# Transposes between the products of the phase that reads them, and attention output scaled by heads on VectorE alone

## The reference, cut to what matters

```
h = rmsnorm(x) * (1 + scale1) + shift1
q_r, k_r, v_r, g_r, q_d, k_d, v_d, gate_r, gate_d = split(h @ w_in)      # gates: sigmoid
branch_r = (silu(g_r) * group_norm(retention(q_r, k_r, v_r))) @ w_ret_out
o_d      = rmsnorm_per_head(diff_attention(q_d, k_d, v_d))               # 8 heads of 128
branch_d = o_d @ w_diff_out
x  = x + gate1 * ((gate_r * branch_r + gate_d * branch_d) @ w_o)
h2 = rmsnorm(x) * (1 + scale2) + shift2
x  = x + gate2 * ((silu(h2 @ w_ffn_gate) * (h2 @ w_ffn_up)) @ w_ffn_down)
y  = rmsnorm(x)
```

## Time and profile before

| | us |
|---|---|
| median of 3 runs | 1375.28 |
| the profiled execution's own time | 1375.61 |
| its span (first to last instruction) | 1373.9 |
| TensorE matmul busy | 1307.0 (95%) |
| VectorE busy | 635.4 (46%) |
| ScalarE busy | 420.0 (31%) |
| GpSimd busy | 179.8 (13%) |
| share of the ending chain on TensorE | 83% |

### The profile page before, as it was taken

How to read it: one execution, slowest core, us unless ns; L and a number is a source line. 1 busy time by engine, 2 the same in 40 slices (tenths; PEclk the granted TensorE clock), 3 DMA queues, 4 the chain that set the end, 5 groups by cost and what they waited for, 6 DMA issues and landing times.

```text
span 1373.9 us, 20027 instructions
## 1 busy us (share of the span) xinstructions
PE 1307.0 (95%) x7974; PEld 1199.1 (87%) x7974; DVE 635.4 (46%) x1001; ACT 420.0 (31%) x642; POOL 179.8 (13%) x189
## 2 busy tenths in 40 slices
PE   4899999999999999998999799899999999999996
PEld 1599887799999999987788798799998999889995
DVE  3734121466657634372898554452224232343245
ACT  5422233344321122213777222242221121212222
POOL 1002000310001011111899200000000000000000
PEclk9999999999999999998999999999999999999998
DMA  9534222143334443452000215111222122221211
GB/s 299 160 103 121 90 64 75 38 154 122 115 130 143 130 121 97 125 188 85 2 2 1 93 62 184 62 62 61 84 69 92 62 69 84 72 82 62 76 46 77
DMA packets 87180, 129.27 MB, mean 94 GB/s; under 512 B 3465, under 2 KB 64386, under 8 KB 86994
## 3 DMA queue, kind: packets, MB, share of 16 engines
q1 hardware_dynamic: 76800, 95.20, 21.3%
q0 software_dynamic: 9104, 32.20, 7.5%
q10 hardware_dynamic: 1218, 1.07, 0.2%
HBM read 117.43 MB, written 4.73 MB: 89 GB/s over the span
## 4 chain that ended last, share of the span: by engine, by line
PE 83%; POOL 6%; DVE 5%; ACT 2%; DMA 2%; issue 1%; DVEq 0%; SPq 0%; ACTq 0%
PE psum L382 50%; PE psum L411 26%; POOL probs L733 3%; POOL probs L739 2%; PE psum L363 1%; DVE ada_acc L1234 1%; DMA x_nat<-in_x_prompt 1%; PE psum L481 1%; PE psum L482 1%; DMA x<-in_x_prompt 1%; PE psum L835 1%; PE psum L833 0%; PE psum L834 0%; DVE hf L524 0%; ACT junk L969 0%
## 5 line engine op out<-in xcount | busy, mean ns | idle before, releaser
L347 DVE TENSOR_TENSOR w_lo<-w_raw,w_hi 128x2048 fp32r<-128x2048 f32 x78 | 178.7, 2291 | 341.5 <-ACT w_hi L342 333.5
L382 PE MATMUL psum<-h_hi,w_lo 128*128 128x320 f32 x1344 | 307.9, 310 | 4.0 <-DVE hf L524 1.4
L382 PE MATMUL psum<-h_lo,w_hi 128*128 128x320 f32 x1344 | 306.8, 309 | 0.0
L382 PE MATMUL psum<-h_hi,w_hi 128*128 128x320 f32 x1344 | 306.8, 309 | 0.0
L382 PEld LDWEIGHTS psum<-h_hi,w_lo 128*128 128x128 f32 x1344 | 225.0, 188 | 5.4 <-issue 4.4
L382 PEld LDWEIGHTS psum<-h_hi,w_hi 128*128 128x128 f32 x1344 | 225.3, 188 | 0.0
L382 PEld LDWEIGHTS psum<-h_lo,w_hi 128*128 128x128 f32 x1344 | 225.1, 188 | 0.0
L342 ACT ACTIVATE w_hi<-w_raw 128x2048 fp32r<-128x2048 f32 x77 | 146.9, 1908 | 209.8 <-PE psum L411 158.5
L411 PE MATMUL psum<-w_lo,h_hi 128*128 128x512 f32 x240 | 93.7, 390 | 0.4 <-ACT mod L1042 0.4
L411 PE MATMUL psum<-w_hi,h_hi 128*128 128x512 f32 x240 | 93.4, 389 | 0.0
L411 PE MATMUL psum<-w_hi,h_lo 128*128 128x512 f32 x240 | 93.4, 389 | 0.0
(11 more groups left out here) (234 smaller groups left out, 1836.3 us busy)
## 6 DMA issues: line engine op xcount, KB each, us to landing
w_raw<-in_w_in SPq DMA_DIRECT2D x32, 1024.0 KB, 5.7
ada_b<-in_w_ada POOLq DMA_DIRECT2D x32, 512.0 KB, 4.0
w_raw<-in_w_ffn_gate SPq DMA_DIRECT2D x11, 1024.0 KB, 5.2
w_raw<-in_w_ffn_up SPq DMA_DIRECT2D x11, 1024.0 KB, 5.2
ada_a<-in_w_ada SPq DMA_DIRECT2D x8, 1024.0 KB, 12.1
w_raw<-in_w_ffn_down SPq DMA_DIRECT2D x8, 1024.0 KB, 4.8
w_raw<-in_w_ret_out SPq DMA_DIRECT2D x4, 1024.0 KB, 4.7
swapped<-qk_d POOLq DMA_DIRECT2D x32, 128.0 KB, 2.5
```

Source lines behind the costliest of these rows:

```text
L347: dve.tensor_tensor(w_lo[s][:, :, :], w_raw[s][:, :, :], w_hi[s][:, :, :].bitcast(F32), ALU.subtract).then_inc(w_lo_done, 1)
L382: last = pe.matmul(bank(4 * par + 2 * j + h, HALF), w[:, k, cs], x[:, k, h * HALF:(h + 1) * HALF], start=(k == 0 and n == 0), stop=(k == K ...
```

## The change

Order: ret_out goes between gate_r and gate_d, in `PHASES`, in `ADA_FIRST` (which modulation columns a phase carries), in the stream of weight loads, in GpSimd's loads of `w_ada` and on each engine; gated_ret, VectorE's evacuation of ret_out, moves with it.

Transposes: all four stages use three pairs of banks, 2 to 7, instead of four. For h, `pe_to_T` stays in front of the products, block k waits for block k-3, and the last wait is for f and f2 of block 5 instead of block 4. For yg, od and h2 a new function issues blocks 0 to 2, and then one block after each of the first five k of tile j = 0 of the first unit. The first two units are written out ahead of the loop over the others. The loops of ScalarE and VectorE for these stages are as they were.

Scaling: GpSimd's share of `scale_head` goes, with the copy and semaphore that released it; VectorE's loop of ten steps now scales a head in each of the first eight and still writes lo[k-2] behind it.

```
-          ("gate_r", 4, "act", "act"), ("gate_d", 4, "act", "act"), ("ret_out", 4, "dve", "dve"),
+          ("gate_r", 4, "act", "act"), ("ret_out", 4, "dve", "dve"), ("gate_d", 4, "act", "act"),
...
+        def tiles_T(pe, which, src, k, pair, diagonals=None):
+
+            for t in range(TILES):
+                out, x = bank(pair + t // 4, P, (t % 4) * P), src[:, t, k * P:(k + 1) * P]
+                last = pe.matmul(out, x, diagonals[:, t, :], start=True, stop=True) if diagonals is not None else \
+                    pe.transpose(out, x, ident[:, :])
+            last.then_inc(n2t[which]["ps"], 1)
...
             for k in range(KT):
-                if k >= 4:
-                    wait_read(k - 4)
...
+                if k >= 3:
+                    wait_read(k - 3)
+                tiles_T(pe, which, src, k, 2 + 2 * (k % 3))
+            wait_read(KT - 3)
+
+        def pe_T_and_dense(pe, which, src, name, hi, lo, diagonals=None, by_block=None):
+
+            q = n2t[which]
+
+            def block(k):
+
                 if by_block is not None:
...
+                    pe.wait_ge(by_block, k + 1)
+                tiles_T(pe, which, src, k, 2 + 2 * (k % 3), diagonals)
+
+            for k in range(3):
+                block(k)
+            pe_wait_unit(pe, name, 0, 0)
+            for j in range(2):
+                for k in range(KT):
+                    if j == 0:
+                        pe.wait_ge(q["lo"], k + 1)
+                    last = T_products(pe, 0, j, k, hi, lo)
+                    if j == 0 and k + 3 < KT:
+                        block(k + 3)
+                if name in ADA_FIRST and j == 1:
+                    last = pe_ada_sums(pe, name, 0, 0)
+                last.then_inc(mm_done, 1)
+            pe_wait_unit(pe, name, 0, 1)
+            pe_T_unit(pe, name, 0, 1, hi, lo)
+            pe_dense(pe, name, pe_T_unit, hi, lo, first=1)
...
-            pool.wait_ge(od_rstd, 1)
-            for h in range(1, DH, 2):
-                scale_head(pool, h).then_inc(od_scaled, 1)
...
-            pe_to_T(pe, "yg", y_nat)
+            pe_T_and_dense(pe, "yg", y_nat, "ret_out", yg_hi, yg_lo)
             pe_dense(pe, "gate_d", pe_T_unit, h_hi, h_lo)
-            pe_dense(pe, "ret_out", pe_T_unit, yg_hi, yg_lo, split=(n2t["yg"]["lo"], 0))
...
-            pe_to_T(pe, "od", o_nat, by_block=(norm["normo"]["scaled"], od_scaled))
-            pe_dense(pe, "diff_out", pe_T_unit, od_hi, od_lo, split=(n2t["od"]["lo"], 0))
+            pe_T_and_dense(pe, "od", o_nat, "diff_out", od_hi, od_lo, by_block=norm["normo"]["scaled"])
...
-            dve.tensor_copy(spare[:, 0:1], rstd[:, 0:1]).then_inc(od_rstd, 1)
             for k in range(DH + 2):
-                if k < DH and k % 2 == 0:
+                if k < DH:
                     scale_head(dve, k).then_inc(norm["normo"]["scaled"], 1)
                 if k >= 2:
                     split_T(dve, "od", od_hi, od_lo, subln_gain, k - 2)
```

More of the change, by code:

```diff
@@ L104 @@
 FIRST, COUNT, READER, BEFORE, START = lay_out_phases()
-ADA_FIRST = {"gate_r": 0, "gate_d": 4, "ret_out": 8, "v_d": 12}
+ADA_FIRST = {"gate_r": 0, "ret_out": 4, "gate_d": 8, "v_d": 12}
 AHEAD = 1
@@ L329, in build @@
         gate_cols_set, gate_T_ps, gate_T_set = sem("gate_cols_set"), sem("gate_T_ps"), sem("gate_T_set")
-        od_scaled, od_rstd = sem("od_scaled"), sem("od_rstd")
         gate_sent, gate_row_in = sem("gate_sent"), sem("gate_row_in")
@@ L370, in pe_ada_sums, with T_products @@
             return sums_over_partitions(pe, par, bank(4 * par + 3, 4, HALF))
+        def T_products(pe, par, j, k, hi, lo):
+            cs = slice(j * P, (j + 1) * P)
+            for n, (w, x) in enumerate(((w_lo[par], hi), (w_hi[par], lo), (w_hi[par], hi))):
+                for h in range(2):
+                    last = pe.matmul(bank(4 * par + 2 * j + h, HALF), w[:, k, cs], x[:, k, h * HALF:(h + 1) * HALF],
+                                     start=(k == 0 and n == 0), stop=(k == KT - 1 and n == 2))
+            return last
         def pe_T_unit(pe, name, i, par, hi, lo, split=None):
             for j in range(2):
-                cs = slice(j * P, (j + 1) * P)
                 for k in range(KT):
@@ L379, in pe_T_unit @@
                         pe.wait_ge(split[0], split[1] + k + 1)
[L380 to L384, removed]
+                    last = T_products(pe, par, j, k, hi, lo)
                 if name in ADA_FIRST and j == 1:
@@ L451, in wait_tile, with pe_dense @@
                 engine.wait_ge(mm_done, ready(name, i, 1, 1))
-        def pe_dense(pe, name, unit, hi, lo, **kw):
-            with pe.Fori(0, COUNT[name] // 2) as i:
+        def pe_dense(pe, name, unit, hi, lo, first=0, **kw):
+            with pe.Fori(first, COUNT[name] // 2) as i:
                 for par in range(2):
@@ L457, in pe_dense @@
                     unit(pe, name, i, par, hi, lo, **kw)
-        def pe_to_T(pe, which, src, diagonals=None, by_block=None):
+        def tiles_T(pe, which, src, k, pair, diagonals=None):
[4 more added lines that the diff above has]
+            last.then_inc(n2t[which]["ps"], 1)
@@ L465, in pe_to_T @@
+        def pe_to_T(pe, which, src):
             q = n2t[which]
-            readers = (q["f"], q["f2"]) if which in SHIFTED else (q["lo"],)
             def wait_read(k):
-                for r in readers:
-                    pe.wait_ge(r, k + 1)
+                pe.wait_ge(q["f"], k + 1)
+                pe.wait_ge(q["f2"], k + 1)
             for k in range(KT):
-                if k >= 4:
-                    wait_read(k - 4)
-                if by_block is not None:
[L477 to L483, removed]
@@ L486, in pe_to_T @@
-            wait_read(5 if which == "yg" else 4)
+                if k >= 3:
[5 more added lines that the diff above has]
+            def block(k):
+                if by_block is not None:
+                    pe.wait_ge(by_block, k + 1)
[16 more added lines that the diff above has]
+            pe_dense(pe, name, pe_T_unit, hi, lo, first=1)
@@ L488, in in_pair @@
         def in_pair(k):
-            return psum[:, 2 * (k % 4) * BANK:2 * (k % 4) * BANK + TOK]
+            pair = 2 + 2 * (k % 3)
+            return psum[:, pair * BANK:pair * BANK + TOK]
         def modulated(which, shift, k, c, cs):
@@ L615, in _ @@
             stream("gate_r", columns(w_in, 6144))
+            stream("ret_out", columns(by_tile["w_ret_out"], 0))
             stream("gate_d", columns(w_in, 7168))
-            stream("ret_out", columns(by_tile["w_ret_out"], 0))
             stream("q_d", columns(w_in, 3072))
@@ L705, in _ @@
             pool.wait_ge(r_out, RH * TILES)
-            for name in ("gate_r", "gate_d", "ret_out"):
+            for name in ("gate_r", "ret_out", "gate_d"):
                 with pool.Fori(0, 2) as i:
@@ L847, in _ @@
             pe_dense(pe, "gate_r", pe_T_unit, h_hi, h_lo)
-            pe.wait_ge(freed["act"], START["gate_d"]["act"])
+            pe.wait_ge(freed["act"], START["ret_out"]["act"])
             pe.wait_ge(y_gated, RH)
-            pe_to_T(pe, "yg", y_nat)
+            pe_T_and_dense(pe, "yg", y_nat, "ret_out", yg_hi, yg_lo)
             pe_dense(pe, "gate_d", pe_T_unit, h_hi, h_lo)
-            pe_dense(pe, "ret_out", pe_T_unit, yg_hi, yg_lo, split=(n2t["yg"]["lo"], 0))
             pe_dense(pe, "q_d", pe_T_unit, h_hi, h_lo)
@@ L938, in _ @@
             pe.wait_ge(norm["norm2"]["scaled"], TILES)
-            pe_to_T(pe, "h2", x1, diag_r)
             tiles = 0
             for third in range(3):
-                pe_dense(pe, f"up{third}", pe_T_unit, h2_hi, h2_lo, split=(n2t["h2"]["lo"], 0))
+                if third == 0:
+                    pe_T_and_dense(pe, "h2", x1, "up0", h2_hi, h2_lo, diag_r)
+                else:
+                    pe_dense(pe, f"up{third}", pe_T_unit, h2_hi, h2_lo)
                 kt = COUNT[f"up{third}"]
@@ L1127, in _ @@
             act_to_T(act, "yg", yg_hi, gn_gain)
+            dense("ret_out", lambda i, par: None)
             dense("gate_d", gate("gate_d", gate_d, KT))
-            dense("ret_out", lambda i, par: None)
             dense("q_d", copy_T("q_d", qk_d, 0, DHD ** -0.5))
@@ L1409, in _ @@
             dve_to_T(dve, "yg", yg_hi, yg_lo, gn_gain)
-            dense("gate_d", lambda i, par: None)
             def gated_ret(i, par):
@@ L1422, in _ @@
             dense("ret_out", gated_ret)
+            dense("gate_d", lambda i, par: None)
             ada_partial("v_d", 0, 0)
```

## The result

Predicted 1383.5 us (range 1379.5 to 1388); measured 1387.15, the median of 4 runs (1385.15 to 1390.14), beside 1375.18 for the kernel before. The ratio is 1.0092 [1.0069, 1.0114]: slower, by 9 to 16 us. The profiled execution took 1385.15 us with a span of 1383.5; on that basis the forecast was 1383.8.

What follows compares the result with a forecast made beforehand. TensorE's products on lines 382 and 411, three quarters of the span, were taken to bound the kernel. The terms +1.1 (h), +0.2 (yg), -4.4 (od) and +11.3 (h2) gave +8.2, so 1383.5 us, range 1379.5 to 1388.

Steps and rivals of the forecast that it cites:

- h2, +11.3: h2 stage: tile 0's products of the first unit end at 919.9 instead of 908.7, 11.3 us later.
- the turn: h2: one round of products, block, f2 and lo takes 3.9 us, five times; bounds 3.6 and 4.2.
- The step that carried it: h2: VectorE's queue is strict FIFO, so lo[k+1] can't pass the waiting f2[k+3] written ahead of it.
- Rival B: h2: no closed wait between engines, TensorE bounds it, +1.6 instead of +11.3; sum -1.5, 1373.8 us; chance 0.06.
- h, +1.1: Before qk_r: the later last wait starts products 1.65 us later, partly won back; +1.1 us, bounds 0.6 and 1.3.
- Rival A: The clock: half clock in h2's turns, or one there and one in yg, adds 4 us: 1387.5; chance 0.15.
- the ring: h2: products k+1 wait for lo[k+1], behind f2[k+3], waiting for block k+3, issued behind products k; 3.9 us each turn.
- yg, +0.2: yg: TensorE starts earlier but waits 1.5 us at L363 for VectorE's partial; sums end at 363.5 against 363.41.
- od, -4.4: od: products start at 766.4 instead of 774.23, tile 0 is read at 777.7 instead of 782.1; 4.4 us less.
- Rival C: od: VectorE, alternating scaling and lo, is the limit and the 4.4 us don't come; sum +12.6, 1387.9; chance 0.05.
- The order of ret_out and gate_d, at nothing: Phase order: ret_out's evacuations lie beside 15 us of products, loads move with their phases; costs nothing.
- the forecast as summed: Whole kernel: the stage terms add to +8.2 us, 1383.5 us, own range 1381.5 to 1386; chance 0.62.

Runs made afterwards that it cites:

- h2 alone: The kernel before with only the h2 transposes put between the products as in the change: 1384.88 us, ratio 1.0066.
- the experiment that I had expected to win 1 to 2 us: The changed kernel with VectorE's partial of ret_out's first unit taken ahead of the yg blocks: 1386.75 us, ratio 1.0079.

## Why the prediction was right, point by point

- **h2, +11.3: right, measured +11.28.** Each part of the turn came as worked out: 3.91 by the terms, 3.89 measured, and 0.98 for the restarted products. From the first diagonal product to tile 1's first the forecast was 29.05 us, and the trace has 29.12 (889.13 to 918.25). The step that carried it, that lo doesn't pass a waiting f2, is shown by the swap of the two (-8.2 us); that h2 makes the loss, by h2 alone (+11.8). Rival B is out. The rule of the Trainium skill (PSUM — Partial Sum Buffer, Engine vs sequencer instructions) that these queues are strict FIFO is what the trace shows: VectorE stands 2.35 us ahead of an lo whose input was ready.
- **h, +1.1: mis-sized, +3.5.** The late start itself was right (1.64 measured, 1.65 forecast), and the next k were to win 0.5 back, since TensorE no longer stood for lo[5]. The step that failed is the rate of the products, which I took as given. The trace has them at half clock, behind stops of 0.92, 0.91 and 1.42 us: 7.00 us for five k instead of 4.63, 2.4 more. The stage took 67.2 to 67.9 in six profiles with the later wait and 64.2 to 65.1 in the seven others. The two values of the others are the clock, too: the second profile of the kernel before has a shorter stretch at half clock among the first products (65.02), and the products up to yg's transposes then took 221.3 us instead of 222.8. Rival A had the mechanism, but put it into h2 and yg. In the ring itself the clock held: six products took 0.98 us in every turn.
- **yg, +0.2: right, +0.12**, with the wait at L363 (now L362) of 1.10 us instead of 1.5. (The working itself gives 363.5 - 363.41, +0.1.) The step behind it, that the partial sets the end, is shown by that wait. That it can't be moved to the front for gain came out of the experiment that I had expected to win 1 to 2 us.
- **od, -4.4: mis-sized, -3.5** (-3.6 to -4.5 in the profiles of the variants; the form before took 70.25, 71.55 and 72.86 us in three profiles, so a miss of 0.9 is within what one and the same form varies by). The forecast had 15.5 us from the gate's transpose to tile 1; it took 16.36, because the first 15 transposes ran at half clock and lo[0] came 0.6 late, and a block between products was at half clock too. Rival C is out: a lo and a head take 1.53 us, and VectorE waits for hi at the end. The term began with the two engines slowing each other down, and that part of it fails: with GpSimd's share kept, the stage is as short.
- **The order of ret_out and gate_d, at nothing: not contradicted.** The stage that holds it is the +0.12 of yg. It was not tried alone.
- **Not foreseen:** the x load, +0.9, which I had at nothing; it goes with a packet of the instruction queue that falls into the load (above). By chance the start of the span (-0.9) and half-clock stretches in attention (-1.8) lay the other way in that profile; both vary in the profiles of one and the same kernel, too (attention 120.55 and 121.61 before).

In the profile the sum was 9.55 instead of 8.2 us, with +2.4 of clock, +0.9 in od and +0.9 of load against -2.7 of chance. So the total came near for a reason of its own (h2, which is 11.3 of it) and by luck besides: 4.2 us of misses, all on the slow side, were made up for in that profile by 2.7 us that had nothing to do with the change. The median shows it: 1387.15 lies outside the 1381.5 to 1386 that I gave the forecast as summed, and where rival A stood (1387.5), though A's half clock was not in the ring. Later, over six runs, the same kernel had 1385.92, beside a kernel before that stood 1.0 higher (1376.17): +9.75, against +8.2 forecast and +12.0 the first time.

## What to carry to other kernels

Before you put a producer's work between its reader's steps, write down the program order of each engine for one step and look for a circle: here TensorE's block k+3, VectorE's f2[k+3], the lo[k+1] written behind it, TensorE's k+1. A loop that runs some steps ahead is free while the producer runs ahead as well, and becomes the path when the producer is paced by the result. Here transposes went best between products that don't read them, where no reader waits for the first: -4.1 us for yg, with the partial moved ahead, against +0.1 between the products of its own reader.

## What the runs showed of the hardware that was not expected

- A late start can be paid twice. A wait one block later moved the products of h by 1.64 us, and four k of them then ran at half clock, 2.4 us more. TensorE had stood 0.92, 0.91 and 1.42 us between groups of five transposes. The stops alone don't settle when the clock falls. With 0.91 and 0.91 it stayed at 1.00 with the last wait on block 4, and fell in the kernel with the partial ahead (0.92, 0.91). With 0.88 and about 1.42 it stayed at 1.00 in one profile of the kernel before and fell to 0.50 a little later in the other.
- The mean granted clock of one kernel on one chip went from 0.981 to 0.988 between runs, and its time with it from 1380 to 1372 us. Parts of 1 to 4 us were told apart by the stage, not by the total.
- The same load of x took 9.4 to 9.6 or 10.5 to 11.1 us, by kernel, and the longer times are those of the profiles in which a 16 KB packet of the instruction queue starts while it runs.
